# Mean and variance of the mLSTM heads: four feature tiles added up on VectorE, one product of ones on TensorE

## What is computed

```python
# ML_HEADS = 4, ML_DH = 512, ML_INNER = 2048
hc, C_T, n_T, m_T = mlstm_chunk_scan(rs(q), rs(k) * (ML_DH ** -0.5), rs(v), ig, lf, C0, n0, m0)
mu = jnp.mean(hc, axis=-1, keepdims=True)
var = jnp.mean((hc - mu) ** 2, axis=-1, keepdims=True)
hn = ((hc - mu) * lax.rsqrt(var + EPS)).reshape(B, T, ML_INNER) * p['ml_norm'][j]
ho = (hn + p['ml_skip'][j] * xc) * jax.nn.silu(z)
return ho @ p['ml_wdown'][j], ...
```

## Time and profile before

| | us |
|---|---|
| median of three timed runs (lowest, highest) | 2151.14 (2150.75, 2154.91) |
| the profiled execution | 2144.44 |
| its span in the trace | 2142.8 |

### The profile page before, as it was taken

How to read it: one execution, slowest core, us unless ns; L and a number is a source line. 1 busy time by engine, 2 the same in 40 slices (tenths; PEclk the granted TensorE clock), 3 DMA queues, 4 the chain that set the end, 5 groups by cost and what they waited for, 6 DMA issues and landing times.

```text
span 2142.8 us, 24212 instructions
## 1 busy us (share of the span) xinstructions
PE 1872.6 (87%) x9666; PEld 1355.4 (63%) x9666; DVE 751.4 (35%) x1632; ACT 412.0 (19%) x641; POOL 180.5 (8%) x274
## 2 busy tenths in 40 slices
PE   6999999978889994999788988988989998887983
PEld 3777777756678884767453644635626776775863
DVE  1244444442322114445644343544434104221114
ACT  3222222321211112111210210310311003100111
POOL 0000000000011111000002011021030000121100
PEclk9999999988989996999898999999999999888996
DMA  8444344362149994211037046064081322568923
GB/s 324 138 139 139 138 138 138 139 227 80 49 160 330 326 306 150 94 39 50 24 132 251 30 141 213 20 207 147 20 284 43 111 64 79 185 235 324 320 96 133
DMA packets 103203, 330.20 MB, mean 154 GB/s; under 512 B 16528, under 2 KB 16528, under 8 KB 102336
## 3 DMA queue, kind: packets, MB, share of 16 engines
q1 hardware_dynamic: 72864, 234.14, 32.1%
q0 software_dynamic: 30240, 94.67, 11.9%
HBM read 275.49 MB, written 70.03 MB: 161 GB/s over the span
## 4 chain that ended last, share of the span: by engine, by line
PE 70%; DVE 12%; DMA 10%; ACT 3%; issue 3%; POOL 1%; DVEq 0%; POOLq 0%; SPq 0%; ACTq 0%
PE ps L515 26%; PE ps L810 11%; PE ps L816 5%; PE ps L616 4%; PE ps L527 3%; DMA arena<-in_c 3%; DMA out_mc_s<-arena 3%; DMA arena<-h_rows,idx 2%; PE ps L537 2%; PE ps L1096 2%; PE ps L633 2%; PE ps L822 1%; PE ps L1042 1%; PE ps L574 1%; PE ps L1052 1%
## 5 line engine op out<-in xcount | busy, mean ns | idle before, releaser
L515 PE MATMUL ps<-hT,ring 128*128 128x288 f32 x1792 | 469.8, 424 | 34.4 <-ACT hT L1161 11.2
L515 PEld LDWEIGHTS ps<-hT,ring 128*128 128x128 f32 x1792 | 354.5, 199 | 143.0 <-issue 13.4
L810 PEld LDWEIGHTS ps<-arena,ring 128*128 128x128 f32 x2048 | 242.2, 198 | 21.0 <-issue 14.4
L810 PE MATMUL ps<-arena,ring 128*128 128x128 f32 x2048 | 243.2, 281 | 6.6 <-DVE arena L1746 5.3
L515 PE MATMUL ps<-arena,ring 128*128 128x288 f32 x768 | 190.1, 411 | 3.8 <-DVE arena L2128 3.8
L515 PEld LDWEIGHTS ps<-arena,ring 128*128 128x128 f32 x768 | 147.9, 193 | 45.6 <-DVE arena L2128 4.2
L1753 DVE TENSOR_TENSOR arena<-ps,arena 128x128 f32<-128x128 f32 x64 | 18.6, 291 | 286.8 <-ACT arena L1267 286.7
L816 PE MATMUL ps<-ring,arena 128*128 128x512 f32 x256 | 116.1, 598 | 0.0
L1042 PE MATMUL ps<-arena 128*32 128x512 f32 x256 | 72.8, 652 | 39.7 <-DMA arena<-in_c 33.4
L479 POOL DMA_DIRECT2D out_mc_s<-arena x128 | 69.1, 541 | 450.1 <-DVE arena L2082 438.1
L2082 DVE SCALAR_TENSOR_TENSOR arena<-arena,xT,ps 128x512 f32<-128x512 f32 x128 | 87.1, 743 | 52.4 <-PE ps L1052 52.4
(11 more groups left out here) (401 smaller groups left out, 2217.9 us busy)
## 6 DMA issues: line engine op xcount, KB each, us to landing
ring<-in_wstream SPq DMA_DIRECT2D x376, 512.0 KB, 5.0
arena<-in_c SPq DMA_DIRECT2D x128, 256.0 KB, 4.4
out_mc_s<-arena POOLq DMA_DIRECT2D x128, 256.0 KB, 4.2
arena<-y_rows POOLq DMA_DIRECT2D x8, 1024.0 KB, 8.4
arena<-in_hg POOLq DMA_DIRECT2D x8, 512.0 KB, 3.9
out_hg_s<-arena POOLq DMA_DIRECT2D x8, 512.0 KB, 2.9
h_rows<-arena POOLq DMA_DIRECT2D x8, 512.0 KB, 3.6
arena<-in_wstream POOLq DMA_DIRECT2D x2, 2048.0 KB, 21.9
```

Source lines behind the costliest of these rows:

```text
L515: mm = pe.matmul(ps[:, 2 * p + half, 0:TH], ring[:, r, c * P:(c + 1) * P], rhs(k)[:, TH * half:TH * (half + 1)], start=(k == 0), stop=(k = ...
L810: mm = pe.matmul(ps[:, n // 2, P * (n % 2):P * (n % 2 + 1)], w[:, P * c:P * (c + 1)], rows[:, c, :], start=(c == 0), stop=(c == DC - 1))
```

## The change

TensorE's two sums take one tile in place of four. The four tiles are added up on VectorE first, in `mx["mu"]`: for the mean by one add behind each of the last three evictions, for the variance by three adds behind the squares. A semaphore that an earlier stage is done with (`scored`, raised 8 times there) tells TensorE that a sum is complete. TensorE no longer waits for the last eviction or the squares themselves, but for these sums.

```diff
+        s["hsum_ready"] = s["scored"]
...
-                pe.wait_ge(pair_free[(hb + 21) % 2].sem, (hb + 21) // 2 + 1)
                 p = use()
-                s["mu_full"].on(wide((2 * p, 2 * p + 1), [ones] * HT, [ml["q"][:, i, :] for i in range(HT)]))
+                pe.wait_ge(s["hsum_ready"].sem, H + 2 * h + 1)
+                s["mu_full"].on(wide((2 * p, 2 * p + 1), [ones], [mx["mu"]]))
                 gate_tile(h, 2)
-                pe.wait_ge(s["sqh_ready"].sem, h + 1)
                 p = use()
-                sqh = shaped(ml["ktok"].rearrange("p a b -> p (a b)")[:, 0:HT * T], HT, T)
-                s["var_full"].on(wide((2 * p, 2 * p + 1), [ones] * HT, [sqh[:, i, :] for i in range(HT)]))
+                pe.wait_ge(s["hsum_ready"].sem, H + 2 * h + 2)
+                s["var_full"].on(wide((2 * p, 2 * p + 1), [ones], [mx["mu"]]))
                 gate_tile(h, 3)
...
                     pair_free[p].on(tt(ml["q"][:, i, 0:TP], ps[:, 2 * p, :], rd[:, 0:TP], ALU.mult))
+                    if i:
+                        dve.wait_ge(pair_free[p].sem, n // 2 + 1)
+                        ins = tt(mx["mu"], ml["q"][:, 0, :] if i == 1 else mx["mu"], ml["q"][:, i, :], ALU.add)
+                        (V if i < HT - 1 else s["hsum_ready"]).link(dve, ins)
...
                 dve.wait_ge(s["sqh_ready"].sem, h + 1)
+                sqh = shaped(ml["ktok"].rearrange("p a b -> p (a b)")[:, 0:HT * T], HT, T)
+                for i in range(1, HT):
+                    ins = tt(mx["mu"], sqh[:, 0, :] if i == 1 else mx["mu"], sqh[:, i, :], ALU.add)
+                    (V if i < HT - 1 else s["hsum_ready"]).link(dve, ins)
                 for i in range(HT):
```

## The result

| | before | changed |
|---|---|---|
| median of 20 runs each, us | 2150.68 | 2133.03 |
| lowest to highest, us | 2143.46 to 2156.98 | 2126.36 to 2151.43 |
| span of the profiled execution, us | 2142.8 | 2126.7 |

The medians differ by 17.65 us. The ratio, which goes by the means, is 0.9925, with a 95% interval of 0.9908 to 0.9942: 16 us faster, between 12 and 20. The forecast was 14.8 us, and 2136 us for the median. The profiled execution of the changed kernel (2128.22 us) was the third fastest of its 20.

The account below looks back on a forecast made before the run. TensorE was busiest, with both products fully on each head's chain of waits while VectorE had room. Four heads at 4.12 us gave 16.5, less 1.7 for clock falls: 14.8 us gain, 2136 us, range 2129 to 2144.

Parts of the forecast that it names:

- The mean: After a head's last eviction: one add on the path, product from 16 records to 4, mean 2.20 us earlier at VectorE.
- They cost nothing: The mean's first two adds fit VectorE's 1.47 us gaps between evictions; without that cover they would cost 1.57 us.
- The variance: Behind the squares: three adds, then Ln waits for its table load, with 0.6 us slack; Ln 4.12 us earlier per head.
- What came back: Head changes: TensorE's gap grows from 2.43 to about 3.0 us; two clock falls in three, one more, 1.7 us back.
- The fall at gate tile 1: Gate tile behind the samples: 11.06 instead of 7.92 us after a 2.71 us gap, cited for longer gaps making falls likelier.
- In front of the down projection: Cited for longer gaps making falls likelier: after 3.79 us the clock fell to 0.68 over 4 us.
- The clock at the mean: Rival: TensorE's idle time before the mean doubles, clock falls, 3.1 us lost per head; gain 2.4 us, 2149; 8%.
- The gain was handed on: Rival said otherwise: sample loop's DMA states come at their own times, only the last head gains; 4.1 us, 2147; 6%.
- The adds fitted between the evictions: Rival said otherwise: adds do not fit or dependent pairs cost more; up to 1.57 us per head, 2142.6; 10%.

Follow-up runs that it names:

- e7: Changed kernel with three adds that nobody reads ahead of the variance's three; stretch 25.34 and 25.35 us in two heads, 26.73 in the other, against 23.34.
- e6: Changed kernel with two 128x576 multiplications that nobody reads ahead of a head's last step, to lengthen TensorE's gap; stretch 24.93 us.
- e0: The kernel before, unchanged, traced a second time; span 2154.0 us against 2142.8 in the first trace.
- e4: Changed kernel with all three adds of the mean behind the last eviction; ratio to the kernel before 1.0014 (0.9994 to 1.0035).
- e3: Changed kernel, but VectorE adds only three tiles for the mean and TensorE takes the fourth itself; median 2130.14 us, ratio to before 0.9913.

## Why the prediction was right

Counted from the end of the last eviction, in us:

| step | predicted | measured |
|---|---|---|
| one add | 0.754 | 0.757 |
| TensorE's idle time before the mean | 1.56 | 1.74 |
| TensorE starts the mean's product | 0.825 | 0.94 |
| gate tile starts | 1.825 | 1.98 |
| mean at VectorE | 2.025 | 2.26 |
| TensorE's wait before the variance | 0.36 | 0.38 |
| Ln starts | 11.75 | 11.91 |
| slack of the adds behind the table | 0.6 | 0.38 |
| first copy for the next head | 23.2 | 23.34 |
| TensorE's gap before the head change | 3.0 | 2.80 |

**The mean.** Right in mechanism: two adds hidden, one on the path, 16 records down to 4. The term was 0.2 us too good (2.20 predicted, 1.98 measured). Half of it is the signal from VectorE: TensorE started 0.14 us after the add's end, where the product of before started 0.05 after the eviction's. The rest is the product: the gate tile started 1.04 us behind it where I had 1.00, and the mean was at VectorE 0.28 us after that where I had 0.20. "They cost nothing" was a little too good as well: the two hidden adds cost the 0.07 us in front of the stretch.

**The variance.** Right: the table load became what Ln waits for, and e7 shows the slack by using it up. It was smaller than predicted since the squares came 0.23 us later, with the mean, and TensorE started 0.15 us behind the last of the three adds. The gain of the whole stretch was 3.98 us per head against 4.12, so 15.9 against 16.5, or 15.6 with the 0.07 us taken off.

**The tables.** Two loads of 1.28 us each, for Ln and for Exp, now lie on the path in each head; Exp's was on it before, Ln's is new. "ScalarE: Activation LUTs" of the Trainium skill, section "Table sets: the hidden batching unit", says that Ln followed by Exp needs one load, since one set has both. This trace differs: it loads before each (1196.54 and 1198.60). One load less would be 1.28 us per head, an estimate by these rows; that was not tried.

**What came back.** Here the step was partly wrong. I put the head changes at one fall more than before, 1.7 us; in the profiled execution it was none of three, and one fewer than before. As a frequency the idea holds at this place, as the table under e6 shows, though how often the changed kernel's other executions fall there is not shown; as a price it was too small, since a fall costs up to 3.0 us. The fall at gate tile 1, which I took as a sign for the length of a gap, is none: it comes there after 1.70 us as well. In front of the down projection the gap grew from 3.79 to 4.04 us, and TensorE ran there at 0.50 and then 0.76, where it had been at 0.68 and 0.89:

```profile
1646.00:1650.00 4.00, 3.91 (x8) 2.86 (x9) 0.03 (x1) 0.00 (x0) 0.54 (x1) 0.50 0.62 198
1650.00:1654.00 4.00, 4.00 (x14) 2.97 (x13) 0.00 (x0) 0.00 (x0) 0.00 (x0) 0.76 0.91 387
```

That is not shown to be the change's doing. The second trace of the kernel before (e0) has 0.50 and 0.84 at this place, after a gap of 3.78 us:

```profile
1668.30:1672.30 4.00, 4.00 (x9) 2.85 (x9) 0.00 (x0) 0.00 (x0) 0.54 (x1) 0.50 0.62 198
1672.30:1676.30 4.00, 4.00 (x15) 3.10 (x14) 0.00 (x0) 0.00 (x0) 0.00 (x0) 0.84 0.90 387
```

So the sum came out nearly right although one of its terms had the wrong sign in the trace that can be read, and to that extent its closeness is luck: 15.9 of the stretches is shown; that the rest of a run averages to nothing is only what the ratio allows.

**The rivals.** The clock at the mean stayed up in the changed kernel: the granted clock from the last eviction to Ln was 1.00 in all four heads, here the first:

```profile
1185.93:1197.84 11.91, 10.59 (x43) 8.10 (x44) 9.68 (x19) 4.06 (x4) 0.00 (x0) 1.00 0.08 22
```

e4's trace shows that it falls, in every head, with an idle time of 3.25 instead of 1.74 us; I had this price at 3.1 us per head, the stretches of e4 lost 1.7, 1.7 and 2.9 beyond the adds' own. The gain was handed on through the sample loop: the three times from a first copy to the next last eviction, 366.8 us together, lie between those of the two traces of before (363.1 and 368.1). The adds fitted between the evictions.

## What to carry to other kernels

Products with ones are cheap to thin out where another engine waits on the same data anyway: an add that fits into a gap of its engine costs next to nothing (0.07 us per head here), one that does not costs its own length and, if TensorE idles longer with it, can cost the clock of what follows, as in e4. Ask of a shortened link what was under its cover; here a table load of 1.28 us took over as what Ln waits for, 0.38 us behind the sums. Where a change leaves TensorE waiting, look for work that does not depend on the wait and move it there: that was worth another 10 us, while what a still shorter link (e3) is worth could not be told from the scatter.

## What was not expected

- TensorE started 0.14 us behind the add that it waited for (1186.73 to 1186.87), but 0.05 behind the eviction in the kernel before. In e3, where it waits for an eviction again, its fourth tile started 0.06 behind that. The same 0.15 us stands between the last add and the product at the variance. What makes up the 0.1 us is open.
- Gaps of nearly one length gave different clocks: none of 3 head changes fell after 2.80 us, 5 of 6 after 2.87 and 2.88, and the same kernel of before fell in its second head change in one trace and in its first in the other. Gate tile 1 began at half clock after 1.70 us already, and always; ahead of it TensorE makes the samples' short products, ahead of a head change a gate tile and eight records of 288 columns. What decides was not settled.
